# Two transformer layers and a hybrid attention layer on one core: order of the rounding work in the last layer and between layers, a first tile in quarters, later table loads, a prepared last mean and a result stored in four pieces per row tile

## The reference

```python
for i in range(2):                        # first block
    h = rmsnorm(x, g[0])
    m = hyena_shortconv_mixer(h, ...) if i % 2 == 0 else pool_mixer(h, ...)
    x = x + rmsnorm(m, g[1])
    h = rmsnorm(x, g[2])
    f = jnp.square(jax.nn.relu(h @ mlp_w1[i])) @ mlp_w2[i]    # 2048 -> 8192 -> 2048
    x = x + rmsnorm(f, g[3])
...
h = rmsnorm_2(x, norm_g) @ w_in           # last layer, 2048 -> 5388
o_mla = mla_mixer(...) * silu(z_mla)      # 8 heads
o_nsa = nsa_mixer(...) * silu(z_nsa)      # 4 heads, three branches
o_mem = memory_mixer(...) * silu(z_mem)   # 4 heads over the memory
x = x + jnp.concatenate([o_mla, o_nsa, o_mem], -1) @ w_out
return rmsnorm_2(x, final_norm_g)
```

## Time and profile before

| what | value |
| --- | --- |
| median of 3 runs | 2354.55 us |
| the profiled execution | 2354.21 us |
| its span in the profile | 2352.4 us |
| TensorE, matmuls | 2337.4 us, 99% |
| TensorE, weight loads | 1932.0 us, 82% |
| VectorE | 1304.2 us, 55% |
| ScalarE | 1081.8 us, 46% |
| GpSimd | 27.0 us, 1% |
| mean of the DMA over the span | 190 GB/s |
| read from HBM | 442.33 MB |

### The profile page before, as it was taken

The page is one execution under the profiler, slowest core; times in us unless marked ns, Lnnn a source line. Parts: engine busy times, 40 slices in busy tenths (PEclk is TensorE's granted clock), DMA queues, the critical chain, the costliest instruction groups (busy, mean ns, idle before and its releaser), DMA issues.

```text
span 2352.4 us, 25298 instructions
## 1 busy us (share of the span) xinstructions
PE 2337.4 (99%) x10945; PEld 1932.0 (82%) x10945; DVE 1304.2 (55%) x1330; ACT 1081.8 (46%) x1174; POOL 27.0 (1%) x46
## 2 busy tenths in 40 slices
PE   9999999999999999999999999999999999999998
PEld 7778788888888888888888888888888888888887
DVE  6655855544544554546864454544544575456654
ACT  6344444544344344354664444344344364444443
POOL 0000000000000000000000000000000010000000
PEclk9999999999999999999999999999999999999999
DMA  8444555655555555555555555555555555644444
GB/s 326 161 161 179 179 198 196 211 183 195 183 212 184 191 188 188 196 180 207 206 197 192 183 192 185 193 186 190 196 180 196 185 177 210 245 161 146 150 153 143
DMA packets 64159, 446.07 MB, mean 190 GB/s; under 512 B 7241, under 2 KB 7572, under 8 KB 12527
## 3 DMA queue, kind: packets, MB, share of 16 engines
q1 hardware_dynamic: 61568, 429.58, 51.6%
q0 software_dynamic: 2336, 14.76, 1.7%
q10 hardware_dynamic: 144, 0.12, 0.0%
HBM read 442.33 MB, written 2.10 MB: 189 GB/s over the span
## 4 chain that ended last, share of the span: by engine, by line
PE 94%; DMA 2%; ACT 2%; DVE 1%; issue 1%; SPq 0%; POOL 0%; ACTq 0%; POOLq 0%
PE P L341 92%; PE P L344 3%; DMA raw<-in_w_i 1%; ACT hi L484 1%; DMA raw<-in_w_z 1%; DVE raw_r L604 1%; ACT EV L510 0%; ACT EV L480 0%; DVE R_m L588 0%; SPq L969 0%; DVE R_h L591 0%; DVE X L591 0%; ACT EV L564 0%; ACT EV L557 0%; ACT R_h L480 0%
## 5 line engine op out<-in xcount | busy, mean ns | idle before, releaser
L604 DVE TENSOR_TENSOR raw_r<-raw,hi 128x2048 fp32r<-128x2048 f32 (+3 forms) x417 | 912.5, 2190 | 946.6 <-ACT hi L484 945.5
L484 ACT ACTIVATE hi<-raw 128x2048 fp32r<-128x2048 f32 (+3 forms) x417 | 763.8, 1833 | 1011.0 <-DMA raw<-in_w_d 388.1
L341 PE MATMUL P<-hi,R_h 128*128 128x512 f32 (+2 forms) x3840 | 1225.0, 393 | 1.5 <-DVE R_h L591 1.1
L341 PEld LDWEIGHTS P<-hi,R_h 128*128 128x128 f32 x3840 | 720.4, 188 | 153.5 <-issue 7.7
L341 PE MATMUL P<-hi,R_f_r 128*128 128x512 f32 x2480 | 776.9, 391 | 0.0
L341 PE MATMUL P<-raw_r,R_h 128*128 128x512 f32 (+2 forms) x1920 | 744.7, 388 | 0.0
L341 PEld LDWEIGHTS P<-hi,R_f_r 128*128 128x128 f32 x2480 | 465.5, 188 | 96.5 <-issue 0.3
L341 PE MATMUL P<-raw_r,R_f_r 128*128 128x512 f32 x1240 | 482.6, 389 | 0.0
L341 PEld LDWEIGHTS P<-raw_r,R_h 128*128 128x128 f32 x1920 | 361.0, 188 | 73.2 <-issue 4.3
L341 PEld LDWEIGHTS P<-raw_r,R_f_r 128*128 128x128 f32 x1240 | 232.9, 188 | 47.5
L344 PE MATMUL P<-ident,EV 128*128 128x128 f32 (+1 forms) x476 | 71.4, 272 | 0.7 <-ACT R_s L480 0.5
(11 more groups left out here) (190 smaller groups left out, 768.4 us busy)
## 6 DMA issues: line engine op xcount, KB each, us to landing
raw<-in_w_u SPq DMA_DIRECT2D x128, 1024.0 KB, 4.8
raw<-in_w_d SPq DMA_DIRECT2D x128, 1024.0 KB, 4.8
raw<-in_w_z SPq DMA_DIRECT2D x46, 1024.0 KB, 4.9
raw<-in_w_i SPq DMA_DIRECT2D x36, 1024.0 KB, 4.8
raw<-in_w_mo SPq DMA_DIRECT2D x16, 1024.0 KB, 4.8
raw<-in_w_o SPq DMA_DIRECT2D x16, 1024.0 KB, 4.8
raw<-in_w_mkv SPq DMA_DIRECT2D x8, 1024.0 KB, 4.7
R_g<-in_rows POOLq DMA_DIRECT2D x6, 1024.0 KB, 5.3
```

Source lines behind the costliest of these rows:

```text
L341: return self.e.matmul(o, l, r, start=start, stop=stop, skip_group_check=True)
L484: self.e.activation(hi, raw, ACT.Copy).then_inc(*self.inc("high_made", ("high", k, d)))
L604: self.e.tensor_tensor(low, raw, hi.bitcast(f32), ALU.subtract).then_inc(*self.inc("low_made", *names))
```

## The change

Six things are changed.

1. **Head.** Three warming matmuls instead of four. The first tile is loaded in four quarters with four semaphores, with blocks of xt between them, where it was loaded in halves; for this tile the split of a quarter is issued before the first column, not behind it. The three tables of the filter are loaded by a step of its own behind `first_norm`, once tile 8 has landed, where they were loaded in `last_rows`.
2. **Between layers.** `quarter(3)` and `gained(0)` come later in `x_columns`.
3. **Gemms of the last layer.** Eight of them, w_i3 to w_i10, get hold="all": no tile is followed by `split_ahead` at its release, and the tile's rounding is issued at the next `take`, behind the step. `cmp_out`, a step of the compressed branch, is moved behind the first head.
4. **Row order of the output product.** The heads come in the order 8 to 11, 0 to 3, 12 to 15, 4 to 7.
5. **The last mean.** `norm_part` sums the first three squares of a row tile beforehand and takes its part of the mean, beside the third quarter; `norm_whole` adds the fourth in one instruction.
6. **Stores.** Four stores of 512 columns (256 KB) for each row tile, in the order of their ends, where two of 1024 columns were.

```diff
-    o["w_o2"] = tile_w(np.concatenate([wo[1024:], wo[:1024]], 0), 512)
+    o["w_o2"] = tile_w(np.concatenate([wo[128 * h:128 * h + 128] for h in HEAD_ORDER], 0), 512)
...
+    def norm_part(self, part, sums, dim, ready, done):
+
+        self.wait_ge(ready)
+        self.e.tensor_reduce(part, sums, AX.X, ALU.add).then_inc(*self.inc("dve_done"))
+        self.wait_ge(self.own)
+        self.ts(part, part, 1.0 / dim, 1e-6, ALU.mult, ALU.add, done)
+
+    def norm_whole(self, s, y, hf, last, part, dim, ready, half_ready, done):
+        self.wait_ge(ready)
+        self.stt(s, last, 1.0 / dim, part, ALU.mult, ALU.add, (done, "mean"))
...
-                        release(j, done[1], hold and q == n - 1)
+                        release(j, done[1], hold == "all" or hold and q == n - 1)
...
             out_of(1)
-            quarter(3)
             first, second = early(0)
             first()
+            quarter(3)
             squares_of(1)
-            gained(0)
             start(1, second)
             fetch(0, (1,))
             fetch(1, (1,))
+            gained(0)
             fetch(2)
...
-    E.warm(b, k, 4, mark("zero"), warmed)
+    E.warm(b, k, 3, mark("zero"), warmed)
...
-    first_block(0, 0, 2)
     first_tile(0, 0)
+    first_block(0, 0, 1)
+    first_tile(0, 1)
+    first_block(0, 1, 1)
+    first_tile(0, 2)
     first_block(0, 2, 2)
-    first_tile(0, 1)
+    first_tile(0, 3)
...
+    def filter_tables():
+        side_load("c6", m.f_w3, a["w_f3"], ("loaded", 8))
...
-    later += [nop, last_rows, half_squares, nop, first_norm]
+    later += [nop, last_rows, half_squares, nop, first_norm, filter_tables]
...
-        banks, done = gemm(name, HH, HL, h_m, 16, 512, steps=2)
+        banks, done = gemm(name, HH, HL, h_m, 16, 512, steps=2, hold="all")
...
+        heads = [lambda h=h: head_step(mla(h)) for h in range(8)]
+        return heads[0:1] + [cmp_out] + heads[1:] + [head_step, over]
...
-                r = rstd(m.SUMA, D, m.R2, [sums[2 * q + t] for q in range(4)], t)
+                c, r = slice(t, t + 1), mark("rstd")
+                E.norm_whole(m.st[:, c], m.st[:, 2 + t:3 + t], m.half[:, c], m.SUMA[:, t, 3:4], m.R4[:, c], D, [sums[6 + t], part_m[t]], half_m, r)
+                E.norm_root(m.st[:, c], m.st[:, 2 + t:3 + t], m.st[:, 4 + t:5 + t], m.R2[:, c], r)
...
-                for q in (2, 0):
+                for q in (3, 0, 2, 1):
                     done_ = mark("stored")
-                    E.store(t, q, [ends[q], ends[q + 1]], done_)
+                    E.store(t, q, ends[q], done_)
```

More of the change, by code:

```diff
@@ L945, in norm_mean, with norm_whole @@
         self.e.tensor_tensor(y, s, hf, ALU.pow).then_inc(*self.inc("pow_done", (done, "pow")))
+    def norm_whole(self, s, y, hf, last, part, dim, ready, half_ready, done):
+        self.wait_ge((done, "mean"))
+        self.wait_ge(half_ready)
+        self.e.tensor_tensor(y, s, hf, ALU.pow).then_inc(*self.inc("pow_done", (done, "pow")))
     def pads(self, free, done):
@@ L2076, in conduct @@
     mask_m = side_load("c12", m.R_f[:, 2048:3328], a["c_mask"], ranks_done)
-    banks, done = gemm("w_i3", HH, HL, h_m, 16, 512, steps=2)
+    banks, done = gemm("w_i3", HH, HL, h_m, 16, 512, steps=2, hold="all")
     flush()
@@ L2233, in over @@
             E.cmp_ready([cmp_m["kv"], list(acc_free)], cmp_m["ready"])
-        return [lambda h=h: head_step(mla(h)) for h in range(8)] + [head_step, over]
+        heads = [lambda h=h: head_step(mla(h)) for h in range(8)]
+        return heads[0:1] + [cmp_out] + heads[1:] + [head_step, over]
     extra += mla_heads()
-    banks, done = gemm("w_i4", HH, HL, h_m, 16, 512, steps=2)
+    banks, done = gemm("w_i4", HH, HL, h_m, 16, 512, steps=2, hold="all")
     flush()
@@ L2245, in conduct @@
     later.append(lambda: qnsa_m.extend(turn_plain(ks4, ms4, 128, 4, m.QNSA[:, 0:4, :], 96, [list(kpe_m), list(blk_m.values())], more=vw_m)))
-    banks, done = gemm("w_i5", HH, HL, h_m, 16, 384, steps=2)
+    banks, done = gemm("w_i5", HH, HL, h_m, 16, 384, steps=2, hold="all")
     flush()
@@ L2252, in conduct @@
     extra += [lambda h=h: head_step(nsa(h, 1)) for h in range(4)] + [cmp_softmax, head_step, head_step, cmp_turned, lambda: cmp_values(0), lambda: cmp_values(1)]
-    banks, done = gemm("w_i6", HH, HL, h_m, 16, 512, steps=2)
+    banks, done = gemm("w_i6", HH, HL, h_m, 16, 512, steps=2, hold="all")
     flush()
@@ L2274, in __getitem__ @@
         def __getitem__(self, g):
-            return [o_m[blocks[self.k0 + 4 * g + h], t] for h in range(4) for t in range(2)]
+            return [o_m[HEAD_ORDER[self.k0 + 4 * g + h], t] for h in range(4) for t in range(2)]
     def heads_of(k0, n, th, tl, after=None):
-        return columns(lambda t, c: ZO[:, t, 128 * blocks[k0 + c]:128 * blocks[k0 + c] + 128], Heads(k0), n, th, tl, th_free=after)
+        return columns(lambda t, c: ZO[:, t, 128 * HEAD_ORDER[k0 + c]:128 * HEAD_ORDER[k0 + c] + 128], Heads(k0), n, th, tl, th_free=after)
     o0_m, parts = heads_of(0, 4, m.OH0, m.OL0)
@@ L2319, in conduct @@
                 E.times_row(xs, xs, m.R_g[:, 512 * g:512 * g + 512], [sums[2 * g + t], gf_m], ym[t, g])
+                if g == 2:
+                    part_m[t] = mark("part")
+                    E.norm_part(m.R4[:, t:t + 1], m.SUMA[:, t, 0:3], D, [sums[2 * q + t] for q in range(3)], part_m[t])
     E.finish(done_)
```

28 lines of the change are left out of this document (16 added, 12 removed).

## The result

The changed kernel takes 2357.80 us, the median of 20 runs (2356.61 to 2358.83), beside 2354.49 us for the kernel before (20 runs, 2353.62 to 2355.95). The ratio is 1.0013, with an interval of 1.0007 to 1.0019: 3.3 us slower, outside the range of the prediction, though within the 0.2% that the prediction took as no difference. The profiled execution took 2357.71 us with a span of 2355.9, against 2354.21 and 2352.4: 3.5 us more in the span.

The account below looks back on a forecast made before the run. TensorE was busy 2337.4 of 2352.4 us, leaving 15.0 us idle, plus warming matmuls, to win. Head 0, layers +1.0, last layer -1.5 and tail -0.6 gave -1.1: 2353.5 us on the median, range 2350.8 to 2355.7.

Parts of the forecast that it names:

- The tables: Filter tables loaded after tile 8: 0 us, since TensorE has no wait between 30.60 and 400 us.
- The head: Kernel start: first product 0.8 us earlier, but the third and fifth tiles stop it; 0 us, bounds -0.8 and +0.3.
- TensorE at 30.6 clearly sooner: Sign of a wrong forecast: TensorE reaches the fifth weight tile, at 30.60 us before, clearly earlier.
- Between the layers: At 402 and 1907 us: second row tile's columns come later, 0.5 us lost at each; together +1.0, bounds +1.2 and -1.5.
- the order would pay: Rival between layers: three waits go (-1.5) and the second row tile's columns are covered; 2351.0 us, chance 0.16.
- The last layer: Late splits in eight gemms and the output product's row order remove waits: -1.5 us, bounds -2.8 and 0.
- The memory heads: Last layer's four memory heads: 0.81 us wait for the softmax copy goes, next head's copy late by 0.25; gain 0.56.
- the start of the output product: New row order avoids the 0.89 us wait for the last memory head; first product 2253.8 against 2254.52, gain 0.75.
- Starved heads: Rival: late low parts make TensorE wait in 17 cycles from 2085 to 2254, 0.3 us each; 2359 us, chance 0.05.
- The tail: After the last matmul: mean shorter by 0.19 and four smaller stores landing sooner; -0.6 us, bounds -0.9 and +0.1.
- The stores' term: Four 256 KB stores from 2347.48, fixed 1.3 plus 0.65 us each: last lands at 2351.4, against 2352.0.
- The rival of stores in series: Rival at the end: each store pays its fixed part in series, +3.3 for -0.6; 2357.4 us, chance 0.02.

Follow-up runs that it names:

- only the later step: The kernel before with an empty step where the change loads the tables, so the filter's steps come one later, loads unmoved: 2354.07 us.
- the version with the gaining parts: The kernel before with the last layer's late rounding, moved step and row order, plus the prepared mean, keeping two stores per row tile: 2351.97 us.
- late tables in the same step: The kernel before with the filter's tables loaded behind tile 8, but in the step of first_norm, so no step comes later: 2356.87 us.

## Why the prediction was wrong

- **The tables, forecast 0: this is the step that failed, and it is 3.4 of the 4.6 us between the two sums of the ledger.** The text said that "behind 30.60 TensorE has no wait before 400 us, so nothing waits for the tiles that come sooner". That is an argument on tiles that come sooner. It did not ask which tiles come later: 2 MB behind tile 8 meet tiles 9 and 10. And it took "no wait" of TensorE for slack, while ScalarE had waited for tiles all along (4.72 and 1.36 us), with the sine and the evacuations behind them in its queue. It also named what is queued behind the tables on POOL, but not what is queued behind a late tile on ScalarE. A rival of that kind was missing. What the runs show in its place: the tables behind tile 8 alone cost 3.6 us, and the change without them is level with the kernel before (-0.2).
- **The price of a stop.** I had priced every wait at its length. In the changed kernel's profile 1.47 us of waiting cost a further estimated 1.7 through the clock.
- **The head, forecast 0 with bounds -0.8 and +0.3; measured +0.86, and +0.9 alone.** The bound named a delay of the stream by three more issues and had it at a third of its size; that the issues make it is not shown. The first product did come 0.47 sooner (6.98), and the new wait near 18 did come, at 19.18. But the fifth tile is not at 30.6. The prediction had called "TensorE at 30.6 clearly sooner" the sign that it was wrong; it is wrong on the other side, since it counted bytes ahead of tile 3 and took their rate as fixed.
- **Between the layers, forecast +1.0: right.** +0.62 and +0.55 in the kernel with this part alone. In the changed kernel 0.57 of the lag is gone by 1940 us, where the profile of the kernel before has a wait of 0.52 on ScalarE's R_s at 1935 and the changed one has none. The kernels with only the later step and with only the tail have none there either, so this is no merit of the order; why the wait comes and goes is open. That the order would pay (rival, 2351.0) falls.
- **The last layer, forecast -1.5; measured -2.1.** The memory heads gave 0.8 (forecast 0.56; the next head was late by 0.26, as estimated), the start of the output product 0.7 (0.75), the evacuation with its neighbours 0.4 (0.2), and 0.2 more ahead of 2208 us (of the kernel before) that had no place in the sum. Starved heads (rival) did not come: there is no wait of each cycle.
- **The tail, forecast -0.6; measured +0.16.** The shorter mean came with its 0.19. The stores' term failed: the fixed part is larger than the 1.3 us that I took from two stores (the first of four landed 2.4 after its issue, not 1.95), and pieces of 256 KB landed 0.6 to 0.9 us apart and not 0.65, with the last issue 0.33 us later than before. The rival of stores in series, worth +3.3, is further off than the forecast. The sentence on the Trainium skill (DMA: Bandwidth & Descriptors, Anatomy of one DMA) gave an estimated 2.6 us for one such store, by a fit that the page states for DMAs issued by GpSimd, while SP issues these; the first landed after 2.4 and the last of the row tile after 3.3, issued behind the three others.
- **Chances.** Within 0.2% had 0.93, and the change is within it. The range to 2355.7 took in the bounds of the terms that I had looked at; the term that mattered had been set at zero without a bound.

What stays open: the parts measured alone add up to +4.3 (3.6 + 0.9 + 1.6 - 2.2 + 0.4) while the change has +3.3; the waits that come and go from one execution to another are of that size, but no run separates them. What decides whether the clock falls at the stop is open too.

## What to carry to other kernels

When a load is moved, list the transfers that it will meet in its new place, and for each of them what stands behind its consumer in that engine's queue; that the busiest engine has no waits says nothing on the slack of the engines that feed it. A term that is set at zero because "nothing waits" needs a bound like any other. Of a change with six parts, run the parts alone: here one lost 3.6 us, one gained 2.2, and the version with the gaining parts is 2.4 us faster than the kernel before.

## What was not expected of the hardware

- **A stop of 1.5 us can cost more than twice its length, and not in every execution.** In the profile of the changed kernel TensorE stood for 1.47 us and the granted clock then fell to 0.54 for 3.7 us. In the profile of the kernel with late tables alone it stood for 2.35 us, and the clock stayed at its upper level of 2.4 GHz:

```profile
57.00:59.00 2.00, 2.00 (x10) 1.64 (x10) 0.77 (x1) 2.00 (x3) 0.00 (x0) 1.00 0.58 246
```

  Over all runs of that kernel the mean granted clock reads 0.999 in five and 0.998 in six, with medians of 2356.8 and 2358.9 us; of the change, 0.999 in nine (median 2357.2) and 0.998 in eleven (2358.1). The kernel with late tables in the same step reads 0.999 in eight runs (2356.5) and 0.998 in three (2358.4). All runs of the other ten kernels, and of the kernel before beside them, read 0.999. So the fall of the clock is seen only in kernels with such a stop between 54 and 60 us, and the length of the wait alone does not say whether it falls.
- **Small first loads start the stream slower.** With quarters of 256 KB and blocks of 128 KB the stretch from 1 to 5 us moved 165 GB/s, with pieces twice as large 219. The two other kernels with these quarters, the head alone and the change, moved 185 and 177.
- **Stores of 256 KB issued 0.4 to 0.5 us apart landed 0.6 to 0.9 us apart**, where two of 512 KB landed 1.3 us apart: no faster in pieces, and the last one is issued 0.33 us later.
